# A smaller descriptor ring, a twelfth expert slot and an earlier query block in a two-block transformer kernel

## What is computed

```python
act = jax.nn.gelu(jnp.einsum('td,tkd->tk', xt, u_tab[et])) * gt
return jnp.einsum('tk,tkd->td', act, v_tab[et])
```

```python
x = layer_norm(ALPHA * x + att, ln1_g[layer], ln1_b[layer])
expert, gate = route(h, w_router, b_router)
ffn = moe_ffn(h, expert, gate, w_gate[layer], w_up[layer], w_down[layer])
x = layer_norm(ALPHA * x + ffn, ln2_g[layer], ln2_b[layer])
```

## Time and profile before

| | us |
|---|---|
| median of three runs | 2091.82 |
| the three runs | 2090.84, 2091.82, 2095.2 |
| profiled execution: span | 2089.1 |
| profiled execution: its own device time | not given by the page |
| gathers, first issue to last issue | 272.2 to 934.6 |
| experts of layer 0, first product of a half step | 1067.4 |
| second attention stage, first product | 1510.82 |
| last expert load of layer 1, issue | 2022.33 |

### The profile page before, as it was taken

The page is one execution under the profiler, slowest core; times in us unless marked ns, Lnnn a source line. Parts: engine busy times, 40 slices in busy tenths (PEclk is TensorE's granted clock), DMA queues, the critical chain, the costliest instruction groups (busy, mean ns, idle before and its releaser), DMA issues. The chain is left out here.

```text
span 2089.1 us, 23422 instructions
## 1 busy us (share of the span) xinstructions
PE 1768.7 (85%) x9328; PEld 914.3 (44%) x9328; DVE 771.6 (37%) x1877; ACT 423.4 (20%) x990; POOL 299.1 (14%) x284
## 2 busy tenths in 40 slices
PE   9999986886766555668999999888799999998886
PEld 7779862553321111124554444233377544442332
DVE  3955176776667777854230000000213300000002
ACT  2481122221222112223121010000123201110001
POOL 0000033453334444440000000000000000000000
PEclk9999998998886876689999999999999999999999
DMA  7236279999999999997789999999944999999996
GB/s 262 93 131 290 101 299 388 409 415 422 422 421 421 421 421 421 421 420 302 292 360 428 426 428 427 426 426 426 423 181 187 412 427 426 427 427 427 427 426 277
DMA packets 78973, 761.80 MB, mean 365 GB/s; under 512 B 8628, under 2 KB 9621, under 8 KB 17542
## 3 DMA queue, kind: packets, MB, share of 16 engines
q1 hardware_dynamic: 41190, 489.34, 56.1%
q0 software_dynamic: 37664, 270.84, 31.5%
HBM read 759.10 MB, written 1.05 MB: 364 GB/s over the span
## 5 line engine op out<-in xcount | busy, mean ns | idle before, releaser
L2584 PE MATMUL bank<-arena 128*64 128x512 f32 x3072 | 684.3, 599 | 55.3 <-DMA arena<-in_w_up 19.6
L1057 PE MATMUL bank<-arena 64*64 64x512 f32 x2032 | 324.6, 794 | 233.7 <-ACT arena L772 233.6
L2584 PEld LDWEIGHTS bank<-arena 128*64 128x64 f32 x3072 | 233.8, 138 | 492.0 <-issue 470.8
L563 POOL DMA_INDIRECT arena<-in_peer_uv,arena x256 | 287.4, 1123 | 631.5 <-PE bank L1057 305.9
L1401 DVE CUSTOM_DVE_ANT_0 arena<-arena 128x1024 f32<-128x1024 f32 x256 | 313.6, 1225 | 171.2 <-DMA arena<-in_peer_uv,arena 168.0
L1057 PEld LDWEIGHTS bank<-arena 64*64 64x64 f32 x2032 | 93.9, 177 | 444.8 <-ACT arena L772 265.7
L2711 DVE TENSOR_TENSOR arena<-arena,bank 128x512 f32<-128x512 f32 x32 | 22.0, 687 | 718.5 <-PE bank L2584 718.5
L822 PE MATMUL bank<-arena 128*128 128x272 f32 (+2 forms) x768 | 145.2, 349 | 0.5 <-ACT arena L596 0.3
L822 PEld LDWEIGHTS bank<-arena 128*128 128x128 f32 x768 | 126.4, 191 | 19.9 <-issue 2.5
L767 ACT ACTIVATE arena<-arena 128x4 f32<-128x4 f32 (+1 forms) x65 | 13.3, 205 | 466.4 <-DVE arena L1401 466.4
L1487 POOL DMA_DIRECT2D arena<-in_w_router x2 | 1.1, 574 | 562.4 <-POOLq L2469 528.0
(11 more groups left out here) (444 smaller groups left out, 1482.9 us busy)
## 6 DMA issues: line engine op xcount, KB each, us to landing
arena<-in_w_up SPq DMA_DIRECT2D x64, 2048.0 KB, 36.9
arena<-in_w_gate SPq DMA_DIRECT2D x64, 2048.0 KB, 32.9
arena<-in_w_down SPq DMA_DIRECT2D x64, 2048.0 KB, 39.0
arena<-in_w_in SPq DMA_DIRECT2D x13, 2048.0 KB, 8.5
arena<-in_w_out SPq DMA_DIRECT2D x2, 4096.0 KB, 17.9
arena<-in_wq SPq DMA_DIRECT2D x4, 2048.0 KB, 13.6
arena<-in_rg_out SPq DMA_DIRECT2D x1, 4096.0 KB, 13.9
arena<-in_peer_uv,arena POOLq DMA_INDIRECT x256, 17.4
```

Source lines behind the costliest of these rows:

```text
L563: nc.gpsimd.indirect_dma_start(SLOT[slot_of[j]], None, d["peer_uv"], bass.IndirectOffsetOnAxis(IDX[:, u % 4, k:k + 1], 0)).then_inc(s_row[ ...
L1057: m = pe.matmul(bank[banks[t][half]][to:to + HALF, :], DIAG[lo:lo + HALF, k + j, :], row[lo:lo + HALF, D + half * 512:D + (half + 1) * 512 ...
L2584: x = pe.matmul(bank[b][j * C:(j + 1) * C, :], operand[:, c, j * C:(j + 1) * C], RING[s % AHEAD][:, c % (DC // 2), j, :], start=(c == 0), ...
```

## The change

The descriptor ring is set to 2 KB, and the columns that this frees go to `arena` (54616 columns). The ring of expert slots has twelve slots; eleven loads are asked for in each attention stage: slot 10 beside slot 4 in the first, and a new order of slots in the second, where slot 6 is asked for at once. The weights of the second attention stage lie in slots 0 to 5, its own tiles in slots 7 to 10. The norm's parameters and the centered tiles of the expert stage lie in slot 6, so SP asks for LG and LB when half step 90 is done, behind the attention weights instead of ahead of them. A region `ahead` in the front stage holds most of the third query block (seven of eight chunks; the eighth lies behind `w_out`), and the block is asked for right behind the second, ahead of the wait on `s_wm`; the gathers' indices move there too. The router's small tiles move from the lasting region to the stage's own (their use is the same), an iota makes 64 columns instead of 128, and two semaphores of the front stage become one with two values.

```diff
+DESCRIPTOR_RING = 2048
+COLS_ALL = 54616
+PACK_ROWS = P // 2
...
     spec = at.take(DC * D)
+    ahead = at.take((DC - 1) * 4 * P + 8 * R + 4)
...
-    WQ = [cut(base, P, DC, 4 * P) for base in (spec, spec + DC * 4 * P, scan, scan + DC * 4 * P)]
+    WQ_PARTS = [[(cut(base, P, DC, 4 * P), 0, DC)] for base in (spec, spec + DC * 4 * P, scan, scan + DC * 4 * P)]
+    WQ_PARTS[2] = [(cut(ahead, P, DC - 1, 4 * P), 0, DC - 1), (cut(scan + DC * D, P, 1, 4 * P), DC - 1, DC)]
+    WQ_CHUNK = [[part[:, c - lo, :] for part, lo, hi in parts for c in range(lo, hi)] for parts in WQ_PARTS]
...
-    IDX = cut(scan + DC * D, P, 4, R).bitcast(U32)
-    EXPS = cut(scan + DC * D + 4 * R, P, 4, R)
+    held = ahead + (DC - 1) * 4 * P
+    IDX = cut(held, P, 4, R).bitcast(U32)
+    EXPS = cut(held + 4 * R, P, 4, R)
...
             def query_weights(k):
-                sp.dma_start(WQ[k], d["wq"][k].rearrange("p (c n) -> p c n", c=DC)).then_inc(s_wq[k], 16)
+                whole = d["wq"][k].rearrange("p (c n) -> p c n", c=DC)
+                for part, lo, hi in WQ_PARTS[k]:
+                    sp.dma_start(part, whole[:, lo:hi, :]).then_inc(s_wq[k], 16)
...
             query_weights(0)
             sp.dma_start(KEYS, d["keysT"]).then_inc(s_keys, 16)
             query_weights(1)
+            query_weights(2)
             sp.wait_ge(s_wm, 4)
-            query_weights(2)
             query_weights(3)
...
-                te.wait_ge(s_wq[k], 16)
+                te.wait_ge(s_wq[k], 16 * len(WQ_PARTS[k]))
...
-ROUTE_COLS = 800
+ROUTE_COLS = 464
...
-        g.iota(iota, pattern=[[1, P]], base=0, channel_multiplier=0, allow_small_or_imprecise_dtypes=True).then_inc(self.s_cst, 1)
+        g.iota(iota, pattern=[[1, PACK_ROWS]], base=0, channel_multiplier=0, allow_small_or_imprecise_dtypes=True).then_inc(self.s_cst, 1)
...
-            experts(4)
+            experts(4, 10)
...
-    return [K.cut(moe_base(K, slots), P, DC, w) for slots, w in ((10, N_DH * HD), (2, N_DH * HD), (4, N_DH * HD + MEM_W))]
+    return [K.cut(moe_base(K, slots), P, DC, w) for slots, w in ((2, N_DH * HD), (4, N_DH * HD), (6, N_DH * HD + MEM_W))]
...
-    return K.cut(moe_base(K, 10) + DC * N_DH * HD, P, DC, T)
+    return K.cut(moe_base(K, 2) + DC * N_DH * HD, P, DC, T)
...
-    at = Room(moe_base(K, 4), moe_base(K, 6))
+    at = Room(moe_base(K, 7), moe_base(K, 9))
...
-    at = Room(moe_base(K, 6), moe_base(K, 7))
+    at = Room(moe_base(K, 9), moe_base(K, 10))
...
-    at = Room(moe_base(K, 7), moe_base(K, 8))
+    at = Room(moe_base(K, 10), moe_base(K, 11))
...
+            experts(6)
             sp.wait_ge(s_pm, VALUE_JOBS)
-            experts(9)
+            experts(1)
             sp.wait_ge(s_pm, job("k", DPAIRS - 1) + 1)
-            experts(0, 1)
+            experts(2, 3)
             sp.wait_ge(s_pm, len(JOBS))
-            experts(2, 3, 8)
+            experts(0, 4, 5)
             sp.wait_ge(s_sm, HEADS)
             sp.wait_ge(s_sc, HEADS)
-            experts(4, 5)
+            experts(7, 8)
             sp.wait_ge(s_om, 4)
-            experts(6)
+            experts(9)
             sp.wait_ge(router.s_mm, LOGITS_MM + TT)
-            experts(7)
+            experts(10)
...
-MOE_SLOTS = 11
-EARLY_SLOTS = 10
+MOE_SLOTS = 12
+EARLY_SLOTS = 11
+PARAM_SLOT = 6
...
-    after = Room(moe_base(K, AHEAD - 1), moe_base(K, AHEAD))
+    after = Room(moe_base(K, PARAM_SLOT), moe_base(K, PARAM_SLOT + 1))
...
-            sp.wait_ge(s_step, more * (PAIRS * HALVES) + (PAIRS * HALVES - (AHEAD - 3)))
-            sp.dma_start(LG, d["ln2_g"][layer].partition_broadcast(P)).then_inc(s_par, 16)
-            sp.dma_start(LB, d["ln2_b"][layer].partition_broadcast(P)).then_inc(s_par, 16)
             if not last_layer:
                 steps = sp.value_load(NSTEPS[0:1, 0:1], min_val=FIRST_FREE, max_val=FIRST_FREE + (PASSES - 1) * (PAIRS * HALVES))
                 names = ("w_v", "w_k", "w_in1")
-                for n, (to, name, later) in enumerate(zip(dilated_weights(K), names, (0, 3, 5))):
+                for n, (to, name, later) in enumerate(zip(dilated_weights(K), names, (0, 2, 4))):
                     sp.wait_ge(s_step, steps + later if later else steps)
                     src = d[name].rearrange("(c p) n -> p c n", p=P) if n == 2 else d[name][0].rearrange("p (c n) -> p c n", c=DC)
                     sp.dma_start(to, src).then_inc(K.s_att_w[n], 16)
+            sp.wait_ge(s_step, more * (PAIRS * HALVES) + (PAIRS * HALVES - (AHEAD - 1 - PARAM_SLOT)))
+            sp.dma_start(LG, d["ln2_g"][layer].partition_broadcast(P)).then_inc(s_par, 16)
+            sp.dma_start(LB, d["ln2_b"][layer].partition_broadcast(P)).then_inc(s_par, 16)
...
-        K.cols = 50900
+        K.cols = COLS_ALL
...
-    nc = _bacc.Bacc("TRN2", target_bir_lowering=False, num_devices=1)
+    nc = _bacc.Bacc("TRN2", target_bir_lowering=False, num_devices=1, dynamic_dma_scratch_size=DESCRIPTOR_RING)
```

More of the change, by code:

```diff
@@ L975, in queries @@
                     for c in range(DC):
-                        m = pe.matmul(bank[b][:, j * P:(j + 1) * P], WQ[k][:, c, j * P:(j + 1) * P], XT[t][:, c, :],
+                        m = pe.matmul(bank[b][:, j * P:(j + 1) * P], WQ_CHUNK[k][c][:, j * P:(j + 1) * P], XT[t][:, c, :],
                                       start=(c == 0), stop=(c == DC - 1))
@@ L1480, in __init__ @@
         self.SUMW, self.GWB = (cut(at.take(2 * NE), P, 2 * NE) for _ in range(2))
-        self.LGT = cut(at.take(TT * NE), P, TT, NE)
+        self.LGT, self.SEL, self.OH = (cut(at.take(TT * NE), P, TT, NE) for _ in range(3))
+        self.PAIR = cut(at.take(8 * 6), P, 8, 6)
+        self.GS8, self.M8, self.E8F, self.G8 = (cut(at.take(16), P, TT, 8) for _ in range(4))
+        self.E8, self.GI8 = (cut(at.take(16), P, TT, 8).bitcast(U32) for _ in range(2))
+        self.GRPF = cut(at.take(2), P, 2)
         self.s_in, self.s_cst = sem("router_in"), sem("router_constants")
@@ L1595, in vector_choose @@
             do(v.max_index(GI8[:, t, :], G8[:, t, :], GS8[:, t, :]))
-        do(v.tensor_copy(K.GRPF, GI8[:, :, 0]))
-        do(v.tensor_tensor(OH, both(self.GRP), wide(K.GRPF), ALU.not_equal))
+        do(v.tensor_copy(self.GRPF, GI8[:, :, 0]))
+        do(v.tensor_tensor(OH, both(self.GRP), wide(self.GRPF), ALU.not_equal))
         do(v.scalar_tensor_tensor(SEL, OH, -BIG, SEL, ALU.mult, ALU.add))
@@ L1602, in vector_choose @@
             do(v.max_index(E8[:, t, :], M8[:, t, :], SEL[:, t, :]))
-        do(v.tensor_copy(K.E8F, E8))
+        do(v.tensor_copy(self.E8F, E8))
         ve.wait_ge(self.s_cst, 4)
-        do(v.tensor_tensor(TMPA, both(K.IOTA[:, 0:NE]), wide(K.E8F[:, :, 0]), ALU.is_equal))
-        do(v.tensor_tensor(TMPB, both(K.IOTA[:, 0:NE]), wide(K.E8F[:, :, 1]), ALU.is_equal))
+        do(v.tensor_tensor(TMPA, both(K.IOTA[:, 0:NE]), wide(self.E8F[:, :, 0]), ALU.is_equal))
+        do(v.tensor_tensor(TMPB, both(K.IOTA[:, 0:NE]), wide(self.E8F[:, :, 1]), ALU.is_equal))
         v.tensor_tensor(MSK, TMPA, TMPB, ALU.add).then_inc(self.s_vec, 1)
@@ L1912, in _ @@
             ve.wait_ge(s_par, 32)
-            do(v.memset(K.GS8, -BIG))
+            do(v.memset(router.GS8, -BIG))
             for t in range(TT):
@@ L2783, in build @@
         route = Room(ROUTE_COLS)
-        K.IOTA = cut(route.take(P), P, P)
+        K.IOTA = cut(route.take(PACK_ROWS), P, PACK_ROWS)
         K.RK, K.GT = (cut(route.take(TT * PASSES * NE), P, TT, PASSES * NE) for _ in range(2))
-        K.PRB, K.MSK, K.SEL, K.OH, K.TMPA, K.TMPB = (cut(route.take(TT * NE), P, TT, NE) for _ in range(6))
-        K.PAIR = cut(route.take(8 * 6), P, 8, 6)
-        K.GS8, K.M8, K.E8F, K.G8 = (cut(route.take(16), P, TT, 8) for _ in range(4))
-        K.E8, K.GI8 = (cut(route.take(16), P, TT, 8).bitcast(U32) for _ in range(2))
-        K.NM_, K.SUMS, K.RS, K.GRPF = (cut(route.take(2), P, 2) for _ in range(4))
+        K.PRB, K.MSK, K.TMPA, K.TMPB = (cut(route.take(TT * NE), P, TT, NE) for _ in range(4))
+        K.NM_, K.SUMS, K.RS = (cut(route.take(2), P, 2) for _ in range(3))
         K.CNT, K.NPF = (cut(route.take(1), P, 1) for _ in range(2))
```

19 lines of the change are left out of this document (10 added, 9 removed).

## The result

The changed kernel takes 2101.06 us (median of 20 executions, 2094.59 to 2105.27) where the kernel before, run beside it, takes 2093.14 (20 executions, 2090.84 to 2099.79). The ratio is 1.0033, with a 95% interval of 1.0023 to 1.0042: slower by 6.9 us, 4.8 to 8.8. The forecast was 5.8 us more and 2097.6. The profiled execution has a span of 2095.0 and a time of 2096.81; before, the span was 2089.1. In every execution for which both are known, the time is 1.7 to 1.8 us above the span. By that, an estimate, the profiled execution of before took 2090.8 us, as little as the fastest of the 20; that of the changed kernel lies 4 us under its median. Both profiles are thus of short executions, and a few us between them mean little.

What follows compares the result with a forecast made beforehand. The DMA queue was taken to bound the gather and expert plateaus, PE the last valley. Terms -4.9 - 4.9 + 20.5 - 4.9 = +5.8 on 2091.8 gave 2097.6 us, range 2092 to 2104.

Steps and rivals of the forecast that it cites:

- term 1: Gather plateau: third query block loaded ahead of it takes its bytes off a full queue, -4.9 us (bounds 0 and 7.6).
- Term 3: End of layer 0: LG and LB behind the attention weights make DVE wait; second attention stage 20.5 us later.
- Rival (a): LG and LB overtake, landing within 8.6 us of layer 0's last expert load: no +20.5, time 2077.1; chance 0.10.
- Rival (b): A gain is missing: slots set the gather pace, or an extra load displaces another; +10.7, 2102.5 us; chance 0.13.
- Term 2: Layer 0's expert stage: eleventh load asked for early puts every load one place earlier in a full queue, -4.9 us.
- Term 4: Layer 1: slots 6 and 1 loaded ahead of the key products' release leave one load less, -4.9 us.
- the ring of 2 KB: Gathers: smaller descriptor ring costs 0, since from three gathers in flight on the queue stays full.
- rival (c): Ring holds two gathers or fewer, POOL stands at its issue: +62 us, some 2154, far more at one; chance 0.05.
- The marks named ahead: Last load of layer 0 near 1483.5, second attention stage 10 to 11 us later, last load of all near 2076.
- the signs of being wrong: No s_par wait, second attention stage before 1515, gathers over 2.5 us apart without slot waits, or last gather still at 954.

Runs made afterwards that it cites:

- experiments 7 and 9: 7: ring of 512 bytes in the kernel with LG and LB first, ratio 1.0312; 9: query weights loaded three times in the changed kernel, 1.0045.
- Experiments 1 to 3: LG and LB asked for first in the changed kernel, 0.9914; last in the kernel before, 1.0078; between w_k and w_in1 in the changed kernel, 0.9992.
- experiments 10 and 11: Ten loads, not eleven, ahead of layer 0: in the changed kernel, ratio 1.0025; in the kernel with LG and LB first, 0.9939.
- experiment 2: The kernel before with only LG and LB moved behind the three attention weights in SP's list: ratio 1.0078.

## Why the prediction was right, and where it was not

Time, sign and range came out, and the mechanism of the largest term was the named one. That the sum came so near is in part luck: its first term was mis-sized, and others made up for it. In us, with the pair of profiled executions of before and after, and the means over all profiled executions that share the order in question (term 1 without experiments 7 and 9, whose gathers were altered):

| term | forecast | the pair | means |
|---|---|---|---|
| 1, third block: first gather's issue to last landing | -4.9 | +1.4 | -2.2 |
| 2, eleventh load: to the last load of layer 0 | -4.9 | -6.7 | -7.2 |
| 3, LG and LB: to the second attention stage | +20.5 | +20.3 | +19.5 |
| 4, eleventh load: release to the last load of layer 1 | -4.9 | -5.3 | -4.4 |

The pair's span has two parts more: the first gather was issued 1.5 us earlier, and the way from the last load to the end is 2.4 us shorter (16.8, before 19.1). With these, +1.4 - 6.7 + 20.3 - 5.3 - 1.5 - 2.4 = +5.8. The means add up to +5.7. The timed runs split it otherwise: with LG and LB first, the change is worth -18.0 and -16.7 us (0.9914 and 0.9920), where the forecast's other three terms give -14.7, and the order costs 24.9 and 23.2, not 20.5. Both are larger than the terms, and they cancel.

**Term 3** held in every step: the order, LB's landing (28.8 us for 29.1), DVE at its wait (20.14 for 20.5), PE behind it, and no extra price for the clock: the transposes took 3.67 us (3.58 before), the first products 27.79 as before. Experiments 1 to 3 show it from both sides. Rival (a) fell: LG, issued 4.5 us behind w_in1, landed 0.4 us ahead of it, and LB landed 2.5 us behind it, so the small transfers kept, to a few us, the place that SP's list gave them.

**Term 1** is the step that failed: "The queue is full (427 GB/s), so I take what the bytes cost". The row for that was 20 us long, and in it one block was itself in the queue. The next 55 us were not looked at: there the queue ran at 379 GB/s instead of 402, and 1.3 of the 2.1 MB saved are lost again. Rival (b) had named the cause, the pace of the slots, and priced it at nothing left; by the means 2.2 us are left, under half and inside the bounds of 0 and 7.6, though in the pair there is nothing.

**Term 2** was too small at its mark. The prediction counted the load asked for early, which measured 4.1 us there, close to the 4.9, and not the slot that is there besides: with twelve slots and ten loads ahead some 3 us were gained already, and at the start of the expert stage, where this shows, "a full queue" does not hold. That term 2 reaches the end is not shown (experiments 10 and 11).

**Term 4** and **the ring of 2 KB** came out as put, term 4 in the time more clearly than at its mark. The working behind the ring's 0 did not hold: "From three in flight on the queue stays full", but with 2.8 in flight the engines moved 362 GB/s and the time grew by 82 us. What rival (c) describes, POOL at its own issues, is real at a quarter of that size. Its price of 2154 us left out the other terms; with the +10.7 of terms 2 to 4 it would have been some 2165.

The marks named ahead were met in order, not to the microsecond: the last load of layer 0 at 1486.5 (forecast 1483.5), the second attention stage 13.5 us later (10 to 11), the last load of all at 2078.3 (2076). Each is 2 to 3 us late, which fits a first term that is missing from this pair and a second that is larger. Of the signs of being wrong only the last came: the last gather still landed at 954.

## What to carry to other kernels

When a buffer moves to another slot, look at what its load now stands behind in the issuing engine's list: 1 MB of parameters behind 10 MB of weights made DVE wait 20 us, and a free half slot brought it back with all the gains of the change (0.9914 and 0.9920 of before). Price a saved transfer only in the stretches in which the queue is full, and read the stretch behind the one where it was saved as well. A gain of less than 5 us in a kernel whose own executions differ by as much needs several profiled executions, since one of them may be 4 us early by itself.

## What was not expected of the hardware

The same code ran at different speeds from one execution to the next. The first 32 products of layer 0's expert stage took 5.43 us before and 3.80 in experiment 2, whose program up to there is the same. The granted clock was 0.68 from 1062.0 to 1067.4 before, that is part of it at 1.2 GHz, and 1.00 from 1066.2 to 1070.0 in experiment 2. The half step behind a late load shows the same at the end of the program; the changed kernel first, then its repeat:

```profile
2072.32 3.65 PE L2601 MATMUL bank<-arena 128*64 128x512 f32 x16 [1.25 <-DMA arena<-in_w_down]
```

```profile
2073.80 5.01 PE L2601 MATMUL bank<-arena 128*64 128x512 f32 x16 [2.81 <-DMA arena<-in_w_down]
```

Behind 2.81 us of waiting the sixteen products took 1.4 us more; the granted clock over them was 0.72, against 1.00 in the first. These two places are worth 1.4 and 1.6 us.

SP's issue of LG lasted 33.69 us in the changed kernel (33.49 in the repeat, 25.67 in experiment 2), where w_v, w_k and w_in1 just ahead of it were issued in 0.33 to 0.39, and LB could only be issued behind it, at 1499.53. What SP stood for is not shown. LB landed 2.5 us behind w_in1 where its bytes alone are 1.2 us; by that, an estimate, the late issue cost some 1.3 us here.
